# Weight chunks made by quarters during two attentions, and low halves moved behind the next chunk in two output products

## What is computed

```python
for layer in range(DEPTH):                       # DEPTH = 2: layer 0 "even", layer 1 "odd"
    hn = rmsnorm(h, mix_norm[layer])
    if layer % 2 == 0:
        h = h + moba_nsa_mixer(hn, ...)          # ends with  o @ even_w_out
    else:
        h = h + fox_mixer(hn, ...)               # ends with  o @ odd_w_out
    h = h + sqrelu_mlp(rmsnorm(h, mlp_norm[layer]), mlp_w1[layer], mlp_w2[layer])
```

## Time and profile before

| | us |
|---|---|
| median of 3 runs | 1323.95 (1323.13 to 1329.26) |
| the profiled execution, its time | 1324.85 |
| the profiled execution, its span | 1323.1 |
| PE busy | 1241.1 (94%) |
| VectorE busy | 840.8 (64%) |
| ScalarE busy | 655.7 (50%) |
| POOL busy | 236.5 (18%) |

### The profile page before, as it was taken

One profiled execution on the slowest core, in us unless ns is written; L12 is line 12 of the kernel. 1 busy time (PEld: TensorE's weight loads), 2 busy tenths in 40 slices (PEclk: granted clock), 3 DMA queues, 4 the chain that ended last, 5 costly groups with the idle time before them and its releaser, 6 DMA issues.

```text
span 1323.1 us, 19217 instructions
## 1 busy us (share of the span) xinstructions
PE 1241.1 (94%) x7748; PEld 1075.5 (81%) x7748; DVE 840.8 (64%) x1296; ACT 655.7 (50%) x1061; POOL 236.5 (18%) x304
## 2 busy tenths in 40 slices
PE   5998789999999979999999999998999889999996
PEld 5876468888888757888888888998997569888996
DVE  4874557666568358666657776457665766777643
ACT  5323646663433365664446555345545544655531
POOL 4001421120000131111112222002303301122201
PEclk8998899999999989999999999999899969999998
DMA  7591115555453514456454554652451005355461
GB/s 262 175 275 42 64 65 191 189 181 203 161 191 127 223 65 159 171 188 219 187 189 161 182 186 150 203 203 97 157 177 43 1 24 208 127 191 191 143 212 60
DMA packets 34232, 206.61 MB, mean 156 GB/s; under 512 B 3792, under 2 KB 6368, under 8 KB 13792
## 3 DMA queue, kind: packets, MB, share of 16 engines
q1 hardware_dynamic: 34144, 205.39, 44.6%
HBM read 203.92 MB, written 1.46 MB: 155 GB/s over the span
## 4 chain that ended last, share of the span: by engine, by line
PE 80%; DVE 11%; ACT 4%; DMA 1%; POOL 1%; issue 1%; SPq 1%; POOLq 0%; DVEq 0%
PE ps L637 33%; PE ps L642 23%; PE ps L640 6%; PE ps L641 6%; DVE wl L581 3%; PE ps L661 1%; PE ps L663 1%; PE ps L662 1%; PE ps L884 1%; PE ps L950 1%; DMA raw<-wstream 1%; ACT wh L573 1%; POOL pb L969 1%; PE ps L1397 1%; DVE y L1909 1%
## 5 line engine op out<-in xcount | busy, mean ns | idle before, releaser
L581 DVE TENSOR_TENSOR wl<-raw,wh 128x2048 fp32r<-128x2048 f32 (+3 forms) x201 | 435.7, 2173 | 153.7 <-ACT wh L573 153.2
L637 PE MATMUL ps<-xb,wh 128*128 128x512 f32 x1424 | 502.1, 398 | 4.5 <-DVE wl L581 3.1
L642 PE MATMUL ps<-xb,wl 128*128 128x256 f32 x1712 | 483.1, 282 | 0.0
L573 ACT ACTIVATE wh<-raw 128x2048 fp32r<-128x2048 f32 (+3 forms) x201 | 358.0, 1784 | 163.9 <-PE ps L642 121.9
L642 PEld LDWEIGHTS ps<-xb,wl 128*128 128x128 f32 x1712 | 327.3, 191 | 0.0
L637 PEld LDWEIGHTS ps<-xb,wh 128*128 128x128 f32 x1424 | 267.9, 188 | 70.8 <-issue 6.9
L642 PE MATMUL ps<-ab,wl 128*128 128x256 f32 x1088 | 307.0, 282 | 0.0
L637 PE MATMUL ps<-ab,wh 128*128 128x512 f32 x640 | 225.1, 396 | 2.7 <-DVE wl L581 2.7
L642 PEld LDWEIGHTS ps<-ab,wl 128*128 128x128 f32 x1088 | 207.8, 191 | 0.0
L637 PEld LDWEIGHTS ps<-ab,wh 128*128 128x128 f32 x640 | 120.0, 188 | 32.3 <-issue 2.3
L834 DVE TENSOR_TENSOR tf<-ps,tf 128x256 f32<-128x256 f32 x148 | 61.9, 422 | 116.0 <-ACT tf L829 116.0
(11 more groups left out here) (322 smaller groups left out, 1397.4 us busy)
## 6 DMA issues: line engine op xcount, KB each, us to landing
raw<-wstream SPq DMA_DIRECT2D x157, 1024.0 KB, 4.8
raw<-wstream SPq DMA_DIRECT2D x32, 704.0 KB, 4.1
raw<-wstream SPq DMA_DIRECT2D x8, 768.0 KB, 4.3
e_bt<-scratch SPq DMA_DIRECT2D x16, 128.0 KB, 6.9
o_bt<-scratch SPq DMA_DIRECT2D x2, 1024.0 KB, 11.3
raw<-wstream SPq DMA_DIRECT2D x2, 560.0 KB, 10.1
raw<-wstream SPq DMA_DIRECT2D x4, 256.0 KB, 6.2
h<-xt SPq DMA_DIRECT2D x4, 256.0 KB, 6.7
```

Source lines behind the costliest of these rows:

```text
L573: e.g.activation(WH[i % HLN][:, 0:w], RAW[i % RAWN][:, 0:w], ACT.Copy).then_inc(S["hi"], 1)
L581: e.g.tensor_tensor(WL[q][:, 0:w], RAW[i % RAWN][:, 0:w], f32(WH[q][:, 0:w]), ALU.subtract).then_inc(S["lo"], 1)
L637: e.g.matmul(PS[b][:, :].rearrange("p (a t) -> p a t", a=2), wh[:, sl], x2[:, :, cs], start=start, stop=k == p.nk - 1, skip_group_check=pair)
L642: ins = e.g.matmul(o, wl[:, sl], xh[:, cs], start=False, stop=k == p.nk - 1, skip_group_check=pair)
```

## The change

In both attentions, each of the two chunks is made in quarters of 512 columns, one quarter per step. Even loop: ScalarE makes the high quarters in steps 6 to 9 and 12 to 15, VectorE the low quarters in steps 10 to 13 and 16 to 19. Odd loop: high quarters in steps 2 to 5 and 6 to 9, low quarters in steps 6 to 9 and 10 to 13. Only the first high quarter waits for the transfer and for the earlier product, and only the last quarter signals.

In both output products VectorE's drain of a tile no longer makes the low half of `x`. The low halves of two tiles are made together, behind the low half of the chunk whose event comes next; those of the last two tiles follow the additions of the last tile.

```diff
+        def hi_part(e, c, x):
+            w = widths[c] // 4
+            s = slice(x * w, x * w + w)
+            if x == 0:
+                e.wait_ge(S[f"w{c % RAWN}"], landed(c))
+                e.wait_ge(S["gemm"], end_of[c - HLN])
+            ins = e.g.activation(WH[c % HLN][:, s], RAW[c % RAWN][:, s], ACT.Copy)
+            if x == 3:
+                ins.then_inc(S["hi"], 1)
+                e.split = c + 1
+        def lo_part(e, c, x):
+            w = widths[c] // 4
+            s, q = slice(x * w, x * w + w), c % HLN
+            e.wait_ge(S["hi"], stream_no(c, 15))
+            ins = e.g.tensor_tensor(WL[q][:, s], RAW[c % RAWN][:, s], f32(WH[q][:, s]), ALU.subtract)
+            if x == 3:
+                ins.then_inc(S["lo"], 1)
+                e.split = c + 1
@@ dve_gemm
-        def dve_gemm(e, p, behind, after=None, drain=None, ahead=2, first=None):
+        def dve_gemm(e, p, behind, after=None, drain=None, ahead=2, first=None, between=None):
             for kind, i in p.events:
                 if kind == "chunk":
                     lo_to(e, min(i + 2 - behind, p.first + p.chunks - 1 + ahead))
+                    if between and i > p.first:
+                        between(e, i - p.first)
@@ act_even
-                if i in (10, 16):
-                    hi_to(e, G["eo"].first + (i - 10) // 6)
+                if 6 <= i < 10 or 12 <= i < 16:
+                    hi_part(e, G["eo"].first + i // 12, i % 6)
@@ dve_residual
                 e.g.tensor_tensor(h, ps[:, 0:T], h, ALU.add).then_inc(ready, 1)
-                dve_split(e, n, k)
+                if k == KT - 1:
+                    behind_chunk(n)(e, KT // 2)
+        def behind_chunk(n):
+            def f(e, c):
+                for k in (2 * c - 2, 2 * c - 1):
+                    dve_split(e, n, k)
+            return f
@@ dve_even
-                if i in (11, 17):
-                    lo_to(e, G["eo"].first + (i - 11) // 6)
+                if 10 <= i < 14 or 16 <= i < 20:
+                    lo_part(e, G["eo"].first + i // 16, (i - 10) % 6)
...
-            dve_gemm(e, G["eo"], 1, drain=dve_residual(G["eo"], S["h_eo"], 1))
+            dve_gemm(e, G["eo"], 1, drain=dve_residual(G["eo"], S["h_eo"], 1), between=behind_chunk(1))
@@ act_odd
-                if i in (5, 10):
-                    hi_to(e, G["oo"].first + i // 5 - 1)
+                if 2 <= i < 10:
+                    hi_part(e, G["oo"].first + (i - 2) // 4, (i - 2) % 4)
@@ dve_odd
-                if i in (6, 11):
-                    lo_to(e, G["oo"].first + i // 5 - 1)
+                if 6 <= i < 14:
+                    lo_part(e, G["oo"].first + (i - 6) // 4, (i - 6) % 4)
...
-            dve_gemm(e, G["oo"], 1, drain=dve_residual(G["oo"], S["h_oo"], 3))
+            dve_gemm(e, G["oo"], 1, drain=dve_residual(G["oo"], S["h_oo"], 3), between=behind_chunk(3))
```

## The result

The changed kernel takes 1307.85 us (median of 4 runs, 1303.89 to 1312.4) against 1325.21 us of the kernel before on the same chip: a ratio of 0.9882, 95% interval 0.9854 to 0.991 (the ratio stands for 15.6 us, the two medians for 17.4). The profiled execution took 1304.75 us with a span of 1303.0 us.

What follows compares the result with a forecast made beforehand. PE was taken to bound the kernel, with gains where it waits for VectorE. Attentions 18.5 - 9.6 - 3.0 = 5.9 us plus products 3.86 make 9.8: 1324.85 to 1315.1, median 0.9 lower, 1314.2 us; range 1309.0 to 1321.5.

Steps and rivals of the forecast that it cites:

- products, both: Output products: PE's three waits for VectorE's low half go, 1.93 us in each product, 3.86 us in both.
- what can go in the loops: Attention loops: 20.6 us over the undisturbed pace for four chunks, less a tenth for other things: 18.5 us.
- low quarters, 16: Attention loops: each of VectorE's sixteen low quarters costs 0.6 us, 9.6 us in all.
- high quarters, 16: Attention loops: ScalarE's sixteen high quarters cost nothing, since ScalarE waits or the quarter is covered.
- falls of the clock that stay: Attention loops: three falls to 1.2 GHz behind chunks were kept, 1.0 us each, 3.0 us in all.
- E: Rival, output products: no gain, because PE at once waits for something else; 1318.1 us, chance 0.08.
- The room of 0.5 us: Output products: VectorE's loop falls to 5.31 us against PE's 5.82, so what is late next has 0.5 us of room.
- the two ends given: Attention loops: price of a low quarter, 0.26 us from below and 1.03 us from above.
- D: Rival, attention loops: quarters stand in line at every pair's step, 1.94 us each; 8.6 us slower, 1332.6 us, chance 0.07.
- rival B: Attention loops: no fall of the clock behind a chunk, 3.0 us more gain, 1311.2 us; chance 0.15.
- The 1.0 us that was worked out for one: Attention loops: cost of one clock fall, 6.7 us at 1.2 GHz holding 1.32 pairs that would otherwise take 5.7 us.
- C: Rival: clock stays at 1.2 GHz through both attention loops, 3.2 us lost, 3.86 won in products; 1323.3 us, chance 0.18.

Runs made afterwards that it cites:

- the third execution: The changed kernel, unaltered, run once more beside its two halves on one chip: median 1308.89 us, ratio 0.9885 to the kernel before.
- the third experiment: Against the changed kernel, loops make whole chunks again, each high half one step earlier, products as changed; ratio 0.9983 to the kernel before.

## Why the prediction was right, and where its sum was wrong

The direction and the places came out; the size didn't. The gain was 9.8 us by the sum and is 16.9 by the same steps with their sizes in the two profiled executions.

| step | predicted | measured |
|---|---|---|
| products, both | 3.9 | 5.0 |
| what can go in the loops | 18.5 | 17.3 |
| low quarters, 16 | -9.6 | -5.4 |
| high quarters, 16 | 0 | 0.0 |
| falls of the clock that stay | -3.0 | 0.0 |
| sum | 9.8 | 16.9 |

The 17.3 are the 20.6 us of the prediction less the 3.28 that stay without chunks. Against executions with whole chunks other than the profiled one the gain is smaller: the mean of that and the two with the products alone is 32.61 and 23.40 us in the loops, which leaves 6.6 + 3.8 + 5.0 = 15.4 us. The three measurements of the changed kernel gave 17.4, 14.1 and 18.0 us by the medians, 15.6, 12.3 and 15.3 by the ratios.

**Products.** The mechanism was right: PE's waits for the low half are gone, and E with them. The term was mis-sized, because PE's busy time of 23.27 us was taken for PE's own work. Without a stop that work takes 22.70 us; each stop cost PE its idle time of 0.65 us and then some of its busy time. The room of 0.5 us that was seen on VectorE isn't there: the step took 5.31 us for its loop, and the rows show 5.67 with no idle time marked, since the two low halves of `x` take 1.84 us beside POOL's sums, 0.88 more than 2 x 0.48, and the chunk's low half gives back only 0.56 of it. It cost nothing here only because PE is as long. That tile 6 comes later doesn't show (the stretch behind `eo` went from 254.47 to 254.62 us, and is 254.19 and 254.68 with the products alone).

**Low quarters.** The length was right (0.67 and 0.68 us against 0.69). The price of 0.6 us was too high by nearly half: 0.34, between the two ends given and near the lower one of 0.26, which was made from the free time of VectorE. The step that failed is "I take 0.6, nearest to the row of the quarter itself": that holds at the even loop's steps that open a chunk (0.60 and 0.77), not at the odd loop's (0.29), and was applied to all. At odd steps POOL is held up as predicted, but by 0.39 us, and most of this finds room. Pairs of two quarters came to 3.87 to 4.21 us, against the 4.3 of the forecast.

**High quarters.** Taken at nothing, and measured at 0.03 and 0.02 us a loop. D, which needed them in line with the low ones, falls with this: ScalarE's quarter ahead of an exponential isn't on the path.

**The clock.** This is the other step that failed, and here rival B was right for the profiled execution. Three falls behind chunks were kept. With the cheaper quarters PE is busy for 2.94 of 4.00 us in a pair, and the clock held behind all chunks in the profiled execution, in the second one of the changed kernel, in one of the two of quarters alone, and in that without low quarters. It isn't certain: in the third execution a stretch at 1.2 GHz began at 160.2 us, 3.85 us behind step 22, and made the loop's end 1.7 us and `eo` 0.6 us longer. Four of the seven executions with low quarters in the loops have it: this one, one of quarters alone, that with the second low half in the product and that without high quarters. PE's work ahead of it doesn't tell them apart. Behind step 22, columns as in the stages, the third execution and then the profiled one:

```profile
156.40:160.00 3.60, 2.16 (x18) 1.19 (x18) 2.14 (x13) 2.76 (x11) 2.31 (x5) 1.00 0.01 2
160.30:167.00 6.70, 5.96 (x26) 3.94 (x27) 0.98 (x2) 2.07 (x2) 0.35 (x1) 0.50 0.01 2
...
156.20:159.80 3.60, 2.16 (x18) 1.19 (x18) 2.13 (x13) 2.77 (x11) 2.32 (x5) 1.00 0.01 2
```

What decides between the two isn't shown here. Whole chunks had two or three falls behind chunks in each of four executions. So it was right not to count on the falls to vanish, but three was too many: it is none or one, of 2.3 to 2.7 us. The 1.0 us that was worked out for one also rests on a wrong reading: the pair of 5.06 us from 162.17 to 167.23 ran at 1.2 GHz only until 165.9.

**C.** The Trainium skill, TensorE: Matmul & The Clock Gate, section A second HAM failure mode: psum-queue depth-cycling, says that short idle stretches between groups of matmuls make the clock swing. This case's traces agree in part. PE has nine waits for POOL of up to 0.7 us in the odd loop's five pairs, and the granted clock is 1.00 in every pair; behind step 22 of the even loop its waits are no longer than 0.85 us, and there the clock fell in four executions of seven. What went ahead of the falls in the kernel before were the long stops, and with the 3.00 us stop of the third experiment they came back. C's 1.2 GHz through both loops came in none.

## What to carry to other kernels

When a loop waits for a big piece of side work, look at what its engine blocks besides itself, and cut the piece to a size that fits the loop's free time; better, move it to a stage where that engine has time and PE has work, which here was worth another 7.4 us by the medians, 5.8 of them in the twelve pairs. Price a piece at the step where it stands: one on the path can cost its whole length, one beside a wait costs a part. Take PE's own work from a stretch without a stop, not from the busy time of one with stops.

## What the hardware showed that I had not expected

**Who starts first holds up the other, VectorE or POOL.** With POOL's sum 0.04 us ahead, VectorE's subtraction took 2.84 us instead of 2.28 and the sum its 0.74; with the subtraction 0.08 us ahead, the subtraction took 2.28 and two sums 3.68 us. The Trainium skill, SBUF — State Buffer, section SBUF: two separate sides, says that an exclusive lock decides this for a VectorE operation with two inputs in SBUF, for the whole instruction, by who comes first; the trace agrees with both numbers. So POOL's busy time in each product rose from 3.70 to 8.92 us, and nothing got slower by it.

**A stop of PE costs more than its idle time.** Three stops of 0.65 us, 1.93 us of idle time in a product, made it 2.49 us longer, all at a granted clock of 1.00.

**The clock ahead of the change differs from one execution to the next.** The same changed kernel began its even loop at 106.16, 110.69 and 106.46 us, with a mean clock of 0.978, 0.969 and 0.974 over the run, and its spans lie 10 us apart, where the pairs repeat to 0.1 us. A change of this size is read more surely from its stages than from a few times.
